# Expert layer of a hybrid decoder step on one core: down products two chunks behind the up products, across the bounds between experts

## What is computed

```
def _swiglu(x, wg, wu, wd):
    return (jax.nn.silu(x @ wg) * (x @ wu)) @ wd

def _moe(x, router, router_b, wg, wu, wd):
    ...
    logits = (xt @ router).astype(F32) + router_b
    top_v, top_i = lax.top_k(logits, TOP_K)
    top_w = jax.nn.softmax(top_v, axis=-1)
    gate = jnp.sum(jax.nn.one_hot(top_i, N_EXPERTS, dtype=F32) * top_w[..., None], axis=1)
    y = jnp.zeros((B * L, D), F32)
    for e in range(N_EXPERTS):
        y = y + gate[:, e:e + 1] * _swiglu(xt, wg[e], wu[e], wd[e])
```

## Time and profile before

| what | us |
|---|---|
| median of 3 runs (1863.24 to 1865.34) | 1863.38 |
| the profiled execution | 1871.23 |
| its span, first to last instruction | 1869.5 |
| PE busy in the span | 1788.2 |
| DVE busy | 1405.9 |
| ACT busy | 938.1 |

### The profile page before, as it was taken

How to read it: one execution, slowest core, us unless ns; L and a number is a source line. 1 busy time by engine, 2 the same in 40 slices (tenths; PEclk the granted TensorE clock), 3 DMA queues, 4 the chain that set the end, 5 groups by cost and what they waited for, 6 DMA issues and landing times.

```text
span 1869.5 us, 26521 instructions
## 1 busy us (share of the span) xinstructions
PE 1788.2 (96%) x10176; PEld 1512.1 (81%) x10176; DVE 1405.9 (75%) x1695; ACT 938.1 (50%) x975; POOL 15.2 (1%) x32
## 2 busy tenths in 40 slices
PE   7998999999999999899999989999999989999897
PEld 7977889899998978688878767787777868787685
DVE  4958955576655858976668879797898979888795
ACT  4624323243333632522326666665666666666574
POOL 1000000000001000000000000000000000000000
PEclk9979999999999979999979999999999999999999
DMA  6523312354452622321628879797888979889780
GB/s 261 203 70 113 107 69 103 115 218 181 181 188 80 215 87 95 109 112 66 251 79 306 344 263 346 303 341 302 298 343 309 336 272 339 331 335 345 264 315 23
DMA packets 59595, 402.81 MB, mean 215 GB/s; under 512 B 8704, under 2 KB 9376, under 8 KB 11600
## 3 DMA queue, kind: packets, MB, share of 16 engines
q1 hardware_dynamic: 54432, 393.73, 56.5%
q0 software_dynamic: 1600, 3.97, 0.6%
q10 hardware_dynamic: 3440, 3.41, 0.5%
HBM read 396.60 MB, written 4.49 MB: 215 GB/s over the span
## 4 chain that ended last, share of the span: by engine, by line
PE 80%; DVE 11%; ACT 4%; issue 3%; DMA 1%; POOL 0%; DVEq 0%; ACTq 0%; SPq 0%; POOLq 0%
PE mA L2141 49%; PE mW L2141 29%; ACT WH L761 2%; DVE slots_rounded L1492 1%; PE mA L2065 1%; DVE SCR L1337 1%; DVE SQ L1422 1%; PE mW L2144 0%; DMA slots<-in_w_in_dram 0%; DVE V L1923 0%; DVE SCR L1651 0%; DVE SQ L1899 0%; DVE BIG L1720 0%; DVE SQ L1902 0%; DVE HEL L1267 0%
## 5 line engine op out<-in xcount | busy, mean ns | idle before, releaser
L1140 DVE TENSOR_TENSOR ring_low<-ring,WH 128x2048 fp32r<-128x2048 f32 x216 | 493.1, 2290 | 93.9 <-ACT WH L761 93.3
L761 ACT ACTIVATE WH<-ring 128x2048 fp32r<-128x2048 f32 x212 | 405.0, 1913 | 77.3 <-PE mW L2141 64.0
L2141 PE MATMUL mA<-XH,slots_rounded 128*128 128x264 f32 x1696 | 364.0, 291 | 2.6 <-DVE SCR L1404 2.6
L2141 PE MATMUL mA<-WH,XEH 128*128 128x512 f32 x704 | 295.8, 420 | 8.6 <-DVE XEL L1216 7.0
L2141 PEld LDWEIGHTS mA<-XH,slots_rounded 128*128 128x128 f32 x1696 | 279.8, 190 | 8.6 <-issue 4.7
L2141 PE MATMUL mA<-WH,XEL 128*128 128x512 f32 x704 | 278.7, 396 | 0.0
L2141 PE MATMUL mA<-ring_low,XEH 128*128 128x512 f32 x608 | 241.6, 397 | 0.0
L2141 PE MATMUL mA<-XL,slots_rounded 128*128 128x264 f32 x672 | 193.1, 287 | 0.0
L2141 PEld LDWEIGHTS mA<-WH,XEH 128*128 128x128 f32 x704 | 134.1, 190 | 40.1 <-DVE ring_low L1140 11.1
L2141 PEld LDWEIGHTS mA<-WH,XEL 128*128 128x128 f32 x704 | 133.7, 190 | 32.1
L932 ACT ACTIVATE BIG<-mA,half 128x264 f32<-128x264 f32 x64 | 30.8, 481 | 208.4 <-PE mA L2141 208.3
(11 more groups left out here) (442 smaller groups left out, 3154.9 us busy)
## 6 DMA issues: line engine op xcount, KB each, us to landing
ring<-in_moe_dram SPq DMA_DIRECT2D x216, 1024.0 KB, 4.8
slots<-in_w_in_dram SPq DMA_DIRECT2D x58, 1024.0 KB, 4.8
more_ring<-in_moe_dram SPq DMA_DIRECT2D x48, 1024.0 KB, 4.8
slots<-in_ffn_up_dram SPq DMA_DIRECT2D x22, 1024.0 KB, 5.0
slots<-in_ffn_down_dram SPq DMA_DIRECT2D x12, 1024.0 KB, 4.8
slots<-in_w_branch_dram SPq DMA_DIRECT2D x8, 1024.0 KB, 4.8
slots<-in_w_out_dram SPq DMA_DIRECT2D x8, 1024.0 KB, 5.0
con<-in_const_dram SPq DMA_DIRECT2D x1, 1441.5 KB, 14.3
```

The source lines that it names most:

```text
L761: nact.activation(WH[:, HI_SLOT[j % PAIR], :], expert_slot(j), ACT.Copy).then_inc(weights_hi, 1)
L1140: v.tensor_tensor(expert_low(j), expert_slot(j), WH[:, HI_SLOT[j % PAIR], :].bitcast(F32), ALU.subtract)\
L2141: return nc.tensor.matmul(out, w, x, start=start, stop=stop, skip_group_check=True)
```

## The change

The order of tiles is made anew. In step `c` (2 to 12), TensorE does both up tiles of chunk `c`, turns the hidden values of chunk `c - 1` and adds down of chunk `c - 2`. Steps 11 and 12 take chunks 0 and 1 of the next expert as their up tiles, in the next pair too. Chunks 0 and 1 of the first expert are done ahead of the loop, and down 0 stands between the two up tiles of chunk 3, once the last expert's result has been kept. Scatter and add move to steps 3 to 6, placing to step 7, turning the placement to the end of step 8, the second half of the gather and the first turn of rows to the end of step 9, the second turn into step 10. VectorE's two remainders of tokens stand in step 10, the first ahead of the step's weight tiles, the second behind `HEL`. `HI_SLOT` stays as it is, and now its places 31 to 36 hold the next expert's first tiles and downs 9 and 10. The number of matmuls, roundings, remainders and DMAs is the same. `scatter` itself, two plain fp32 matmuls a part, is the same code in both.

The list of tiles:

```diff
+def next_chunk(u, c):
+    return (0, u, c) if c < FC else (u, 1 - u, c - FC)
+
+def chunk_steps(u, last):
+    for c in range(2, FC + 2):
+        x = next_chunk(u, c)
+        x = None if last and x[0] else x
+        ups = [x + (part,) for part in range(2)] if x else []
+        yield c, ups[0:1] + [(0, u, 0, 2)] * (c == 3) + ups[1:2] + [(0, u, c - 2, 2)] * (c >= 3)
...
+    seq = [(0, 0, c, part) for c in range(2) for part in range(2)]
     for u in range(2):
-        for c in range(FC):
-            seq += [(u, c, 0), (u, c, 1)]
-            if c:
-                seq.append((u, c - 1, 2))
-        seq.append((u, FC - 1, 2))
+        for c, items in chunk_steps(u, last):
+            seq += items
```

ScalarE (the instructions of tanh, `bend`, and of `HEH`, `keep_turned`, are those of before, as functions):

```diff
+            def bend(m, u, c, up):
+
+                b = (FC * u + c) % 2
+                act.wait_ge(*used(m, up))
+                act.wait_ge(hidden, (2 * m + u) * FC + (c + 1))
+                nact.activation(ETH[:, b, :], mA[:, b, 0:256], ACT.Tanh, scale=0.5).then_inc(tanh_done, 1)
...
+                    for c, items in chunk_steps(u, last):
+                        x = next_chunk(u, c) + (1,)
+                        at = [pos(item, last) for item in items]
+                        up = pos(x, last) if x in items else -1
+                        ahead = [j + AHEAD for j in at if more or j + AHEAD < PAIR]
+                        if c == 10 and more:
+                            keep_rows(n + 1, 1)
+                            round_tokens(n + 1, 1 - u, 0)
+                        for j in ahead:
+                            if j - AHEAD < up:
+                                round_weights(m, j)
+                        if c == 9 and more:
                             act.wait_ge(scattered, n * KT + KT)
                             keep_rows(n + 1, 0)
...
+                        if up >= 0:
+                            bend(m, u, c, up)
+                        if up >= 0 or c == FC:
+                            keep_turned(m, u, c - 1, last and u)
+                        if c == 10 and more:
+                            round_tokens(n + 1, 1 - u, 1)
+                        for j in ahead:
+                            if up <= j - AHEAD < at[-1] or j - AHEAD == at[-1] and c < FC + 1:
+                                round_weights(m, j)
+                    act.wait_ge(*used(m, pos((0, u, FC - 1, 2), last)))
+                    nact.activation(YE, WF[:, 0:1024], ACT.Copy).then_inc(down_kept, 1)
                     if more:
+                        round_weights(m, at[-1] + AHEAD)
```

VectorE (`gate` holds a chunk's two products, L1282 and L1285 of before):

```diff
+            def gate(m, u, c):
+
+                b, g = (FC * u + c) % 2, (2 * m + u) * FC + (c + 1)
+                dve.wait_ge(tanh_done, g)
+                v.scalar_tensor_tensor(ETH[:, b, :], ETH[:, b, :], 1.0, mA[:, b, 0:256], ADD, MUL).then_inc(gated, 1)
+                dve.wait_ge(gated, g)
+                dve.wait_ge(hidden_turned, g)
+                v.tensor_tensor(HT[:, b, :], ETH[:, b, :], mA[:, b, 256:512], MUL).then_inc(hidden, 1)
...
+                        if 3 <= c < 7:
+                            add(n, 2 * (c - 3))
+                        if c == 7 and more:
                             place_tokens(n + 1)
                             place_gates(n + 1)
+                        if c == 9 and more:
                             turned(n + 1, 1 - u)
+                        if c == 10 and more:
+                            split_tokens(n + 1, 1 - u, 0)
+                        for j in ahead:
+                            if j - AHEAD < up:
+                                split_weights(dve, v, m, j)
+                        if up >= 0:
+                            gate(m, u, c)
+                        if up >= 0 or c == FC:
+                            split_turned(m, u, c - 1)
+                        if c == 10 and more:
+                            split_tokens(n + 1, 1 - u, 1)
+                        for j in ahead:
+                            if j - AHEAD >= up and not (c == FC + 1 and j == ahead[-1]):
+                                split_weights(dve, v, m, j)
                     if more:
+                        split_weights(dve, v, m, ahead[-1])
```

TensorE:

```diff
+                    for c, items in chunk_steps(u, last):
+                        if 3 <= c < 7:
                             pe.wait_ge(down_kept, n + 1)
...
+                            scatter(n, 2 * (c - 3), PGT[:, 1 - u, :])
+                        for item in items:
+                            part = item[3]
+                            if part == 2:
+                                if item[2] == c - 2:
+                                    turn_hidden(m, u, c - 1) if c < FC + 1 or more else None
+                                    if c == 10 and more:
+                                        turn_rows(n + 1, 1)
+                                down(m, u, item[2], last)
+                            else:
+                                gate_up(m, u, c, part, pos(item, last))
+                        if c == 2:
+                            turn_hidden(m, u, 1)
+                        if c == 8 and more:
                             pe.wait_ge(scatter_added, n * 4 + 5)
                             turn_placement(n + 1)
                             gather_rows(n + 1, 0)
...
+                        if c == 9 and more:
+                            gather_rows(n + 1, 1)
+                            turn_rows(n + 1, 0)
```

More of the change, by code:

```diff
@@ L1269, in experts @@
-                    for c in range(FC):
-                        b = (FC * u + c) % 2
-                        if c:
-                            split_turned(c - 1)
-                        if 2 <= c < 6:
-                            add(n, 2 * (c - 2))
-                        if c == 6 and more:
+                    for c, items in chunk_steps(u, last):
+                        x = next_chunk(u, c) + (1,)
+                        up = pos(x, last) if x in items else -1
+                        ahead = [j for j in (pos(item, last) + AHEAD for item in items) if more or j < PAIR]
+                        if 3 <= c < 7:
+                            add(n, 2 * (c - 3))
+                        if c == 7 and more:
@@ L2051, in moe_tensor, with turn_hidden, down, gate_up @@
             pe.sem_inc(hidden_turned, 2)
+            def turn_hidden(m, u, c):
+                pe.wait_ge(hidden, (2 * m + u) * FC + (c + 3))
+                b = (FC * u + c) % 2
+                for q in range(2):
+                    ins = nc.tensor.transpose(mA[:, 2 + b, P * q:P * q + P], HT[:, b, P * q:P * q + P], C("ident"))
+                ins.then_inc(hidden_turned, 1)
+            def down(m, u, c, last):
+                n, j, b2 = 2 * m + u, pos((0, u, c, 2), last), (FC * u + c) % 2
+                if c == 0:
+                    pe.wait_ge(down_kept, n + 1)
+                pe.wait_ge(turned_lo, n * FC + (c + 1))
+                pe.wait_ge(weights_lo, m * PAIR + (j + 1))
+                wh, wl = WH[:, HI_SLOT[j % PAIR], :], expert_low(j)
+                for q in range(2):
+                    for h, w in ((HEH, wh), (HEH, wl), (HEL, wh)):
+                        for b in range(2):
+                            ins = mm(mW[:, b, :], h[:, b2, P * q:P * q + P], w[:, D * q + 512 * b:D * q + 512 * b + 512],
+                                     c == q == 0 and h is HEH and w is wh, c == FC - 1 and q == 1 and h is HEL)
+                ins.then_inc(weights_used, 1)
+            def gate_up(m, u, c, part, j):
+                n, t, out = 2 * m + u + c // FC, (u + c // FC) % 2, mA[:, (FC * u + c) % 2, :]
+                if c % FC == 0:
+                    pe.wait_ge(gather_split, 2 * n + (part + 1))
+                pe.wait_ge(weights_lo, m * PAIR + (j + 1))
+                wh, wl = WH[:, HI_SLOT[j % PAIR], :], expert_low(j)
+                for k in range(4):
+                    for x, w in ((XEH, wh), (XEH, wl), (XEL, wh)):
+                        ins = mm(out, x[:, t, 4 * part + k, :], w[:, 512 * k:512 * k + 512],
+                                 part == k == 0 and x is XEH and w is wh, part == 1 and k == 3 and x is XEL)
+                ins.then_inc(weights_used, 1)
+            for c in range(2):
+                for part in range(2):
+                    gate_up(0, 0, c, part, 2 * c + part)
+            turn_hidden(0, 0, 0)
             tail = last_pair(pe)
```

160 lines of the change are left out of this document (42 added, 118 removed).

## The result

The changed kernel takes 1822.23 us (median of 4 runs, 1819.22 to 1824.55), the kernel before beside it 1864.36 (1863.24 to 1870.45): a ratio of 0.9769, interval 0.9751 to 0.9788. A second set of runs, beside a before of 1867.09, gave 1821.23 and 0.9757 (0.9734 to 0.9779). So the medians differ by 42 to 46 us; 45.3 were forecast.

What follows compares the result with a forecast made beforehand. TensorE's work was taken to set the pace, with 48.6 us lost at the bounds between experts. Less 1.7 for loop jumps and 1.6 for remaining waits, 45.3 off 1863.4 gave 1818 us; range 1811 to 1838.

Steps and rivals of the forecast that it cites:

- that walk: VectorE's queue in step 10, from a pair's first expert to its second: XEL's second half on time or 0.5 us late.
- the idle time of 0.86: TensorE's gap where the loop over pairs goes back, 0.86 us, stays; two jumps are 1.7 us that don't go.
- the low spells: TensorE at 1.2 GHz after waits between the two experts of each pair; 3.4 us lost at each of four, 13.6.

Runs made afterwards that it cites:

- e1: Changed kernel with VectorE making both halves of XEL behind step 10's weight tiles, not ahead of them; 1864.65 us, ratio 1.0001 to the kernel before.
- e4: Kernel before with HEL of chunk 10 and XEL's first half ahead of a weight tile on VectorE at an expert's end; 1849.60 us, ratio 0.9933.
- e3: Changed kernel with downs 9 and 10 ahead of the next expert's up tiles, still two chunks behind; 1873.32 us, ratio 1.0057 to the kernel before.

## What to carry to other kernels

Where engines hand tiles round in strict queues, walk the queue of the second busiest engine item by item at the seam, with durations from the trace, and compare what is ready with what is asked for: that walk was right within 0.3 us, while sums over busy shares can't see the seam at all. Put the item that the critical engine asks for next ahead of work whose own input waits for that engine, or the two wait for each other; here the whole gain was lost without it (e1), though the order alone, in the kernel before, gave only 16 of the 45 us (e4). Count a wait on TensorE at more than its length where slow matmuls follow it, and judge small edits by distances between like instructions in one profile when the runs scatter by more than the edit is worth.

## What was not expected of the hardware

- A loop's jump back costs TensorE 1.5 us in a stage where nothing else is idle, more than the idle time of 0.86 that the trace showed for it where other waits stood nearby. It is no fixed price: in e3 the idle time at the two jumps is 2.23 and 4.09 us.
- Adding 188 matmuls of no use made the kernel before faster by 0.24% (interval 0.12 to 0.37%), as the low spells behind four waits went.
- Two executions of one kernel can differ almost wholly ahead of the stage that was changed. The two profiles of the changed kernel differ by 2.2 us in their span (1819.1 and 1816.9) and by 2.1 in the start of the expert stage (974.95 and 972.84); the stage itself takes 821.5 us in both. Over all profiles the start lies between 972.5 and 980.2, though no kernel here changes what stands ahead of it on TensorE. Just ahead of it TensorE runs at the lower level, 1.2 GHz, in every profile (granted 0.50 from 968 to 974 us), but the differences are older: 2.2 us between those two by 810 us already, and 3.6 of the 5.2 between the kernel before and the changed one by 945. What makes them was not tried.
